# Ordering VectorE, ScalarE and GpSimd by due times in a two-layer GLA and pooling kernel

## What is computed

```python
def gla_chunk_step(S, chunk):
    ...
    o = jnp.einsum('bhij,bhjv->bhiv', A, vf) + jnp.einsum('bhid,bhdv->bhiv', qf * jnp.exp(b), S)
    S_new = jnp.exp(bC[:, :, 0, :])[..., None] * S + jnp.einsum('bhjd,bhjv->bhdv', kd, vf)
    return S_new, o

def run_layer(h, prompt, S0, buf, norm_g, w_in, w_alpha, ...):
    xn = rmsnorm(h, norm_g)
    z = xn @ w_in
    q, k, v, ga, u, gb, alow, mg = jnp.split(z, IN_OFFSETS, axis=-1)
    la = jax.nn.log_sigmoid(alow @ w_alpha + b_alpha) / GATE_TAU
    ...
    o, S_new = gla_scan(q, k, v, la, S0, ...)
    y_pool = pool_mix(u, ...)
    o = o * lax.rsqrt(jnp.mean(o * o, axis=-1, keepdims=True) + EPS)
    o = o * gla_gain
    o = o * jax.nn.silu(ga)
    ya = o @ w_a
    yb = (y_pool * jax.nn.silu(gb)) @ w_b
    s_a, s_b = jnp.split(jax.nn.sigmoid(mg + b_merge), 2, axis=-1)
    return h + (s_a * ya + s_b * yb) @ w_out, S_new, buf_new
```

## Time and profile before

| | |
|---|---|
| median of 3 runs | 1135.14 us |
| lowest, highest | 1133.49, 1327.73 us |
| the profiled execution | 1134.99 us |
| its span (core 0, the slowest) | 1133.5 us |
| spans of cores 0 to 7 | 1133.5, 1128.9, 1128.9, 1133.1, 1130.5, 1125.7, 1127.7, 1132.5 us |
| mean granted TensorE clock, core 0 | 0.991 |
| busy TensorE, VectorE, ScalarE, GpSimd | 1090.3, 671.4, 516.2, 612.2 us |
| instructions | 27743 |

### The profile page before, as it was taken

The page is one execution under the profiler, slowest core; times in us unless marked ns, Lnnn a source line. Parts: engine busy times, 40 slices in busy tenths (PEclk is TensorE's granted clock), DMA queues, the critical chain, the costliest instruction groups (busy, mean ns, idle before and its releaser), DMA issues.

```text
span 1133.5 us, 27743 instructions; the slowest of 8 cores (1125.7 to 1133.5 us)
## 1 busy us (share of the span) xinstructions
PE 1090.3 (96%) x9886; PEld 857.1 (76%) x9958; DVE 671.4 (59%) x1083; ACT 516.2 (46%) x1052; POOL 612.2 (54%) x929
## 2 busy tenths in 40 slices
PE   6899998999999999999989999999999999999996
PEld 3587776776888777877757877877788867877785
DVE  5457766746544765565453776565656366656554
ACT  2545565665333334334337466555554323433333
POOL 5259787856863333343342787877777323333232
PEclk8999999999999999999999999999999999999998
DMA  9955666665398899889578234355555966745521
GB/s 195 198 110 140 139 94 134 147 144 135 57 228 158 263 273 276 237 241 269 158 141 192 48 85 81 77 97 107 108 92 142 199 201 230 248 173 173 200 83 57
DMA packets 124362, 179.34 MB, mean 158 GB/s; under 512 B 82512, under 2 KB 89168, under 8 KB 120128
## 3 DMA queue, kind: packets, MB, share of 16 engines
q1 hardware_dynamic: 108960, 141.52, 42.0%
q0 software_dynamic: 15264, 36.05, 21.4%
HBM read 140.13 MB, written 54.59 MB: 172 GB/s over the span
## 4 chain that ended last, share of the span: by engine, by line
PE 84%; DMA 5%; issue 3%; POOL 3%; ACT 2%; DVE 2%; SPq 0%; POOLq 0%; DVEq 0%; ACTq 0%
PE psum L561 84%; DMA arena<-w 3%; ACT arena L588 2%; POOL arena L603 2%; DMA arena<-hin 2%; DVE arena L615 1%; DMA arena<-arena 1%; DVE arena L603 1%; POOL arena L610 1%; PE psum L567 0%; SPq L640 0%; ACT L588 0%; POOL arena L635 0%; POOL arena L622 0%; DVE arena L610 0%
## 5 line engine op out<-in xcount | busy, mean ns | idle before, releaser
L561 PE MATMUL psum<-arena 128*128 128x256 bf16 (+6 forms) x9782 | 1085.6, 278 | 34.1 <-DVE arena L615 8.5
L561 PEld LDWEIGHTS psum<-arena 128*128 128x128 bf16 (+2 forms) x9854 | 850.9, 98 | 264.4 <-issue 21.0
L603 POOL TENSOR_TENSOR arena<-arena 128x256 bf16<-128x256 f32 (+12 forms) x349 | 351.4, 1013 | 298.3 <-DVE arena L615 227.7
L615 DVE SCALAR_TENSOR_TENSOR arena<-arena,psum 128x256 f32<-128x256 f32 (+7 forms) x472 | 266.1, 600 | 198.6 <-PE psum L561 129.1
L588 ACT ACTIVATE arena<-psum,arena 128x256 f32<-128x256 f32 (+3 forms) x432 | 173.3, 457 | 303.0 <-PE psum L561 243.9
L588 ACT ACTIVATE arena<-psum 128x256 bf16<-128x256 f32 (+6 forms) x258 | 159.3, 631 | 187.6 <-PE psum L561 160.6
L610 POOL TENSOR_SCALAR arena<-arena 128x256 f32<-128x256 f32 (+6 forms) x378 | 168.3, 454 | 112.3 <-ACT arena L588 63.2
L588 ACT ACTIVATE arena<-arena 128x1024 bf16<-128x1024 f32 (+4 forms) x144 | 141.5, 996 | 101.3 <-DVE arena L615 52.3
L615 DVE SCALAR_TENSOR_TENSOR arena<-psum,arena 128x512 f32<-128x512 f32 (+6 forms) x195 | 125.0, 656 | 62.5 <-PE psum L561 55.1
L615 DVE SCALAR_TENSOR_TENSOR arena<-arena 128x256 bf16<-128x256 f32 (+4 forms) x124 | 116.2, 945 | 67.4 <-POOL arena L603 61.7
L635 POOL DMA_DIRECT2D arena<-w x106 | 62.9, 595 | 54.2 <-PE psum L561 32.8
(11 more groups left out here) (10 smaller groups left out, 21.8 us busy)
## 6 DMA issues: line engine op xcount, KB each, us to landing
arena<-hin SPq DMA_DIRECT2D x32, 512.0 KB, 5.9
arena<-sgla SPq DMA_DIRECT2D x16, 1024.0 KB, 8.1
nsg_s<-arena SPq DMA_DIRECT2D x16, 1024.0 KB, 6.9
arena<-w POOLq DMA_DIRECT2D x30, 512.0 KB, 15.3
arena<-w POOLq DMA_DIRECT2D x48, 224.0 KB, 5.2
arena<-XN SPq DMA_DIRECT2D x20, 512.0 KB, 5.6
H<-arena SPq DMA_DIRECT2D x16, 512.0 KB, 4.6
arena<-H SPq DMA_DIRECT2D x16, 512.0 KB, 4.8
```

The lines of the kernel that those rows point to most:

```text
L561: return S.add("pe", lambda e: e.matmul(out, lhsT=lhsT, rhs=rhs, start=start, stop=stop, skip_group_check=sgc), r=[lhsT, rhs] + list(also_ ...
L603: return S.add(eng, lambda e: e.tensor_tensor(out=out, in0=in0, in1=in1, op=op), r=[in0, in1], w=[out], cost=c)
L615: return S.add("dve", lambda e: e.scalar_tensor_tensor(out=out, in0=in0, scalar=scalar, in1=in1, op0=op0, op1=op1), r=r, w=[out], cost=eco ...
```

## The change

Instead of one pass of the planner there are six. After each pass, `latest` goes backwards over the recorded operations and gives each a due time: TensorE's operations are due when the pass started them, and any other operation so early that those which read its result can be on time. In the next pass ScalarE, VectorE and GpSimd (its weight transfers too) take of their ready operations the one with the smallest due time, while TensorE and SyncE still take the one recorded first. Of the six passes the one whose simulated end is earliest gives the order. The first pass ranks as before. Besides, `tt` gets a factor of 0.42 instead of 1.0 where VectorE works on bfloat16 operands alone.

```diff
+    def latest(self, succ, start_t, done_t):
+        ops = self.ops
+        late = [0.0] * len(ops)
+        for i in range(len(ops) - 1, -1, -1):
+            op = ops[i]
+            span = done_t[i] - start_t[i] if op["dma"] else op["cost"] + op["lat"]
+            t = start_t[i] if op["eng"] == "pe" or not succ[i] else 1e12
+            for j, soft in succ[i]:
+                t = min(t, late[j] - (op["cost"] if soft else span))
+            late[i] = t
+        return late
+
     def list_schedule(self):
+        n = len(self.ops)
+        best = None
+        rank = list(range(n))
+        for k in range(6):
+            end, order, late = self.one_pass(rank)
+            if best is None or end < best[0]:
+                best = (end, order, rank)
+            rank = [i if op["eng"] in ("pe", "sp") else late[i] for i, op in enumerate(self.ops)]
+        self.sim_end, order, rank = best
+        self.one_pass(rank)
...
+    def one_pass(self, rank):
...
                 while pend[e] and pend[e][0][0] <= T:
-                    heapq.heappush(avail[e], heapq.heappop(pend[e])[1])
+                    heapq.heappush(avail[e], heapq.heappop(pend[e])[1:])
                 if avail[e]:
-                    st_, idx = T, avail[e][0]
+                    st_, idx = T, avail[e][0][1]
...
-                    heapq.heappush(pend[ops[j]["eng"]], (ready_t[j], j))
+                    heapq.heappush(pend[ops[j]["eng"]], (ready_t[j], rank[j], j))
+        return max(done_t), order, self.latest(succ, start_t, done_t)
...
         def tt(eng, out, in0, in1, op):
-            c = ecost(eng, fsz(out), 1.0, (out, in0, in1))
+            c = ecost(eng, fsz(out), 0.42 if eng == "dve" and F32 not in (out.dtype, in0.dtype, in1.dtype) else 1.0, (out, in0, in1))
```

22 lines of the change are left out of this document (11 added, 11 removed).

## The result

The changed kernel is slower: 1154.26 us (median of 4 runs, 1153.17 to 1158.18) beside 1135.66 us of the kernel before, a ratio of 1.0176 with a 95% interval from 1.0142 to 1.0211. One of the four runs of the kernel before, at 1327.73 us, was an execution of a slower kind and is left out of every ratio. The forecast was 1130.4 with a range up to 1139.

A forecast was written before the change was run, and what follows sets the result against it. TensorE, busy 1090.28 of 1133.5 us, was taken as the bound, leaving 43.2 us of standing to win. From 1134.99, gains of 6.5 (B, C, D, F, G) less 1.9 for one collision gave 1130.4 us, range 1121 to 1139.

The forecast's parts named there:

- D: 200 to 320 us: the wait of 2.34 before 312.88 for a GpSimd cast shrinks, -1.7; later weight transfers priced 0.
- E: 570 to 620 us: one normalisation moves behind some evacuations; taken as 0, bounds 0 and -1.
- first rival: TensorE takes spare matmuls early, then stands for transfer landings, voiding B, C and F (3.9 us): 1134.3 us, chance 0.22.
- A: Opening, 0 to 60 us: no gain, as TensorE waits again at an input load; 0, bounds 0 and -1.4.
- B: 60 to 160 us: pool branch matmuls cover the 1.30 us wait for VectorE before 110.83; -1.3.
- C: 160 to 200 us: key projection matmuls moved ahead cover waits before 175.34 and 178.64; -1.5, bounds 0 and -3.6.
- F: 840 to 925 us: the 1.47 us wait before 856.25 shrinks as GpSimd's multiplication moves behind the pow; -1.1.
- the one term against the change: One new meeting of long GpSimd and VectorE operations in front of TensorE, place not given: +1.9 us.
- G: The end: the last GpSimd addition no longer runs beside VectorE's 128x1024 operation; -0.9.
- The clock: 178 to 182 us: a half clock spell loses 1.7 us; left as is, another -1.7 if it goes.
- The second rival: Slower: GpSimd and VectorE collide before TensorE in each of layer 0's pairs 2 to 7; +6.7, 1141.7 us, chance 0.12.

The follow-up runs named there:

- e4: Kernel before with the new order only in operations 3263 to 6036 (phase change and merge of layer 0): ratio 1.0085.
- e5: e4 with one weight transfer put back to its old place between the two gate multiplications of pair 6: ratio 1.0043.
- e2: Old order for the first 6036 operations, the changed kernel's order from there (layer change on): ratio 1.0126.
- e7: e2 with two of the eight big weight transfers at the layer change moved some 2.5 us later in GpSimd's queue: ratio 1.0009.
- e13: e4 with the store of pair 6's attention output moved ahead of the input load of tile 14 in SyncE's queue: ratio 0.9997.
- e10: Changed kernel with three weight transfers moved: one at the phase change put back, two at the layer change some 2.5 us later: ratio 1.0031.
- e14: Changed kernel with four transfers moved: the three weight transfers of e10 and the store of e13: ratio 1.0008.
- e11: Kernel before with the cost factor 0.42 alone, one pass, rank by index: ratio 1.0215.
- e8: e2 with the fillers ahead of tile 14's normalisation (memsets, two small forget-gate operations) moved back behind it: ratio 1.0113.
- e6: Kernel before with three instructions moved ahead at the layer change, to make tile 14's normalisation some 1.3 us later: ratio 1.0105.
- e12: Changed kernel without the cost factor: six passes with due times, old cost: ratio 1.0104.

## Why the prediction was wrong

The order of reading was right, and the waits it listed did shrink for the most part. What failed is the sum's treatment of transfers: two terms were put at nothing that cost some 21 us together (medians of the cores, 7.4 and 13.4).

- **The transfers moved with the queue (terms D and E).** In D I priced a weight transfer by its own landing: "If this cover is gone, a load issued some 5 us later is a wait of at most those 5 us; I take 0." The runs show that its price is what it does to others. One weight transfer put back near 305 is worth 1.0085 against 1.0043 (e4, e5). Two at the change of layers, 2.5 us earlier or later, are 1.0126 or 1.0009 (e2, e7). And in E I took 0 with the bounds 0 and -1, for one normalisation, where the trace of before had a transposing transfer of 8.3 us beside weights. That was the row to read: this stretch cost 13.4 us (median of the cores).
- **"SyncE issues in the same order"** stands in the first rival, and A says the same. 31 of its 299 instructions had moved, and I didn't look at which. One of them, a store behind a load, was worth 9.7 us (e4, e13).
- **The first rival** has the right mechanism at the wrong place: TensorE took matmuls early and then stood for a landing, not in B, C and F, but behind D, in the merge. Its price of 3.9 us was too small as well.
- **D failed, and the one term against the change is why.** The wait is 2.47 us after 2.34. GpSimd is free earlier, as forecast, but TensorE now waits for VectorE's update of the state, which starts only at 305.30, because the VectorE operation before it ran beside two gate multiplications, now back to back, and took ten times as long as the like one behind it:

```profile
300.51 4.24 POOL L628 TENSOR_TENSOR arena<-arena 128x1024 bf16<-128x1024 bf16 x2
...
300.94 4.10 DVE L640 SCALAR_TENSOR_TENSOR arena<-arena 128x256 bf16<-128x256 f32 x1
304.97 0.41 DVE L640 SCALAR_TENSOR_TENSOR arena<-arena 128x256 bf16<-128x256 f32 x1
```

  Seven of the eight cores show this (4.09 to 4.10 us, and the wait of 2.5). On core 3 the second multiplication starts 0.9 us later, the operation takes 2.01, and the wait is 0.4 to 0.9, near the 0.6 that was forecast. The kernel before has no such operation over 3 us. So one meeting did fall in front of TensorE, as the term of +1.9 had it, though beside a 128x256 operation and not a 128x1024 one. It isn't the cause of the loss: core 3 still waits 3.8 us for the load, and e10 and e14 have the operation at 4.70 us and lose 0.3% and 0.1%. What it costs by itself was not tested.
- **A** was forecast at 0, with -1.4 as its bound; the idling of 0 to 60 went from 11.4 to 9.8 us (medians of the eight cores), at the bound.
- **B, C.** B was forecast at -1.3 and gave -0.7 in the same measure, since two waits of 0.88 and 0.90 us came in at 122.6 and 126.0, the second behind a VectorE operation of 2.72 us beside a gate multiplication. C was forecast at -1.5 and gave -2.8, inside its bound, with the spell of half clock gone too (the granted clock of 160 to 200 is 1.00, 0.96 before). The sum to the end of pair 7 was forecast at -4.5, and the median core is 3.7 us ahead there.
- **F** held: the wait of 1.5 us is 0.25 (medians), where 1.1 of it was to go (by its own terms, 1.6 less 0.4, it is 1.2). **G** shortened the last additions to 0.3 us each, and yet won nothing: two small waits (0.77 and 0.64) took the place of one of 1.10.
- **The clock** was a smaller second loss. On the eight cores it took 6.5 to 11.8 us from the busy time (median 8.9) and 4.7 to 8.0 before (5.7), in part behind the two new waits; the prediction had it at 1.7 for one spell.
- **The second rival** had the right sign and the wrong cause: its meeting came once per core, not in each of six pairs, and it looked for the loss in phase 1, where the kernel is ahead.

## What to carry to other kernels

When a scheduler or a priority moves instructions, list the transfers that moved first, on every queue, and for each what other transfer is in flight beside it, not only who needs its data. In these runs the transposing transfer was quick wherever the next two weight transfers came 1.8 us or more behind it; put such a distance into the planner, or pin the order of the pair, before ranks by need are allowed to reorder bulk loads. In a queue that is issued strictly in order, put a transfer that is ready ahead of one that waits for an engine. When matmuls are pulled ahead, count the cover that is left under each chain of store and load behind them. Look at VectorE wherever GpSimd's long multiplications come to stand back to back. And a planner whose cost for one operation is made truer can produce a slower kernel (e11); that its other errors had been balanced against the old cost is my reading, and no run tests it.

## What the hardware showed that I had not expected

The time of one and the same transposing transfer (128 x 1024 bfloat16, SBUF to SBUF, issued by SyncE, whose issue instruction takes 1.25 us) against when GpSimd issued the next two 512 KB weight transfers, counted from its issue; the third column is the profiled core, the last the eight cores:

```
kernel   first two weights at     took      on the eight cores
e10       +1.82   +2.45 us         3.9 us   3.7 to 4.8
e7        +1.82   +2.45            4.4      3.9 to 4.6
before    +0.25   +1.82            8.3      7.3 to 8.7
e8        +0.08   +0.70           13.4     13.4 to 21.8
e6        -0.45   +1.82           15.2      7.2 to 7.7 on five, 15.2 to 19.0 on three
e12       +0.82   +2.18           18.8      5.9 to 6.6 on three, 12.7 to 19.5 on five
changed   +0.07   +0.70           22.3     17.0 to 22.4
e2        +0.08   +0.70           26.7     18.5 to 26.7
e11       -0.17   +0.45           35.7     27.4 to 35.7
```

From 4 to 36 us, though the data are the same. With the weights 1.8 us behind, all cores are quick; with both within 0.7 us, all are slow. Between these the distance alone doesn't decide: e6 and e12 give two outcomes for one order. In e12's three quick cores the transfers issued ahead of it had landed sooner (the weight before it took 5.2 to 5.5 us, where it took 6.0 to 6.8 on the others). A long transfer also costs only what isn't covered: the next one, of tile 15, took 28.0 to 30.2 us in the kernel before already, with no wait of half a microsecond behind it. That bulk loads beside it make it slower fits what the Trainium skill says on the page "DMA: Bandwidth & Descriptors", section "Queues, rings and completion order": each transfer engine takes turns between the queues that have work, a packet at a time. In the changed kernel's stretch from 575 to 612 GpSimd's queue moved 4.19 MB in 1186 packets, 3.5 KB each, and SyncE's 1.45 MB in 1868 packets, 0.8 KB each, so in a turn about by packets the queue with small ones gets the smaller share; that this is the cause was argued here and not tested.

The same skill's rule on VectorE and GpSimd ("SBUF — State Buffer", "Who interferes with whom"), weighed in the prediction, agrees with the trace after in who is kept out: 3.26 us for the normalisation at 104.64 beside a gate multiplication, 1.37 for its twin at 110.30, and 4.10 for 0.41 in D. Who came first the trace can't settle: at 104.64 VectorE's recorded start is 0.04 us ahead of GpSimd's 104.68, and yet VectorE is the one that is long. In D it kept the wait of 2.5 us alive, and the large losses were elsewhere.
